# Five plain gate-and-up pairs instead of four ahead of the fast product, two of its four token sums on GpSimd, and another order on the queues

## The chip, the cores and the metric

One core of a Trainium2 chip. The metric is the device time of one launch in microseconds (us), as the median of several executions. TensorE multiplies; VectorE (DVE), ScalarE (ACT) and GpSimd (POOL) prepare its operands and take its results out of PSUM; SyncE (SP) issues the weight loads. Each engine works through its own queue in order, and waits on semaphores for the others.

## The reference

Two decoder layers on 512 tokens of width 1024, each layer wrapped by two half-step SwiGLU feed-forward networks (FFN 0 to 3), a convolution and sparse-attention mixer in the first, a gated DeltaNet mixer in the second. Only the FFNs are touched:

```python
def rmsnorm(x, gain):
    return x * lax.rsqrt(jnp.mean(x * x, axis=-1, keepdims=True) + NORM_EPS) * gain

def swiglu(h, w_gate, w_up, w_down):
    return (jax.nn.silu(h @ w_gate) * (h @ w_up)) @ w_down

x = x + 0.5 * swiglu(rmsnorm(x, norm_gain[layer, 0]), w_gate, w_up, w_down)   # D_FF = 2816
```

## The kernel before

Activations lie feature-major: 8 tiles of 128 features by 512 tokens. Each fp32 operand is split into a high part (a copy to fp32r, on ScalarE) and a low part (the difference, on VectorE, `split` and L1499), and each product is three matmuls, high by high, high by low and low by high. Weights come in units of 128 x 1024, four raw buffers deep: `load(n)` waits until the low part of unit n-3 is made.

An FFN has 22 pairs (gate and up, 128 columns of D_FF each), in two halves of 11, each half followed by 8 down units. A pair is computed in one of two ways:

- *plain*: two units (2p and 2p+1) of 8 x 3 matmuls of 512 tokens. The gain is folded into h, and rstd is applied after the product, so plain pairs can begin before rstd is known. `plain_gate` takes the gate product out of PSUM and scales it, `silu` on ScalarE, `plain_up` multiplies in two steps, `a_act` and `a_dve` split the result.
- *fast*: seven instead of eight block products (Strassen's scheme over two halves of features and two of tokens, with gate and up as the two column blocks), 7 parts of 4 x 3 matmuls of 256 tokens. It needs `hn`, the fully normed activations (`hn_dve`, 8 instructions), four sums of them, t_f[0] to t_f[3] (`t_sum`), their high parts t_hi (`t_act`) and low parts t_lo (`t_dve`), the high and low parts of hn itself, written over h_hi and h_lo (`b_act`, `b_dve`, three of each), and for each pair the sums of weights s_f (two on GpSimd, two on VectorE), with the high and low parts of ab, a22, s12 and s43.

`PLAIN` says how many pairs of each FFN are plain: 6, 4, 4, 4. They give VectorE and ScalarE time to make what the fast pairs need. That work is written by hand into the queues at fixed pairs: with `plain` pairs, hn behind the gate of pair plain-4, the t sums behind the gate of pair plain-3, t_lo around pair plain-2. On TensorE the sum of squares for the norm (`square_sum`, L609), which waits for GpSimd's adding up, stands ahead of unit 1 in FFNs 1 to 3 and ahead of unit 3 in FFN 0. ScalarE makes rstd from it (`norm`).

The first fast pair waits for the first part of h_lo (`b_ready`) before its first matmul, and for all four t_lo before its second part:

```python
pe.wait_ge(ab_ready, q + 1)
if new:
    pe.wait_ge(b_ready, 3 * f + 1)
part_product(own, ab_hi_w[ab], ab_lo_w[ab], 0, ...)
pe.wait_ge(s12_ready, q + 1)
if new:
    pe.wait_ge(t_ready, 4 * f + 4)
```

h_hi can be overwritten only when TensorE has read its first half in the last plain unit (`h_read`). t_lo[i] and t_f[i] are the same memory.

Of the kernel before, what the change touches and what calls it, by code (L numbers as in the profile page):

```python
# [10 lines left out]
ALU = mybir.AluOpType  # L11
# [59 lines left out]
PLAIN = (6, 4, 4, 4)  # L71
# [159 lines left out]
def program(nc, A, out):  # L231
    with ExitStack() as ctx:
# [187 lines left out]
        hn_made, tf_made, t_hi_made, t_ready = (sem(n) for n in ("hn_made", "tf_made", "t_hi_made", "t_ready"))  # L420
# [151 lines left out]
        def _(pe):  # L572
# [85 lines left out]
            def plain_pair(f, p):  # L658
# [3 lines left out]
                for u in range(2):  # L662
                    n = gate_unit(f, p) + u
                    bank = prod[:, 2 * (s % 2) + u, :]
                    if 2 * p + u == (1 if f else 3):
                        square_sum(norm_of(f))
# [376 lines left out]
        def _(act):  # L1043
# [92 lines left out]
            def t_act(f, i):  # L1136

                act.wait_ge(tf_made, 4 * f + (1, 2, 4, 3)[i])
                act.activation(t_hi[:, i], t_f[:, i], ACT.Copy, scale=-1.0 if i == 1 else 1.0).then_inc(t_hi_made, 1)
# [21 lines left out]
            def ffn_act(f):  # L1161
# [6 lines left out]
                for p in range(plain):  # L1168
# [3 lines left out]
                    if p == plain - 2:  # L1172
                        t_act(f, 2)
                    silu(f, p)
                    if p + 1 == plain:
                        break
                    if f or p:
                        split(n + 3)
# [3 lines left out]
                    a_act(f, p)  # L1182
                    if p == plain - 3:
                        t_act(f, 3)
                    if p == plain - 2:
                        ab_act(f, plain)
                        a22_act(f, plain)
                b_act(f, 0)
                s12_act(f, plain)
                for half in range(2):  # L1190
                    end = (half + 1) * HALF
                    for p in range((plain, HALF)[half], end):
                        s43_act(f, p)
                        if p == plain:
                            b_act(f, 1)
                        elif p != HALF:
                            a_act(f, p - 1)
                        snap_act(f, p, 0)
                        if p == plain:
                            b_act(f, 2)  # L1200
                            a_act(f, p - 1)
# [282 lines left out]
        def _(dve):  # L1484
# [103 lines left out]
            def t_sum(f, i):  # L1588


                if i == 0:
                    dve.wait_ge(hn_made, KT * (f + 1))
                    ins = dve.tensor_tensor(t_f[:, 0], hn[0][:, :, tokens(0)], hn[0][:, :, tokens(1)], ALU.subtract)
                elif i == 1:
                    dve.wait_ge(tf_made, 4 * f + 1)
                    ins = dve.tensor_tensor(t_f[:, 1], hn[1][:, :, tokens(1)], t_f[:, 0], ALU.add)
                elif i == 3:
                    ins = dve.tensor_tensor(t_f[:, 3], hn[1][:, :, tokens(1)], hn[0][:, :, tokens(1)], ALU.subtract)
                else:
                    dve.wait_ge(tf_made, 4 * f + 2)  # L1600
                    ins = dve.tensor_tensor(t_f[:, 2], t_f[:, 1], hn[1][:, :, tokens(0)], ALU.subtract)
                ins.then_inc(tf_made, 1)

            def t_dve(f, i):

                dve.wait_ge(t_hi_made, 4 * f + (1, 2, 4, 3)[i])
                dve.scalar_tensor_tensor(t_lo[:, i], t_f[:, i], -1.0 if i == 1 else 1.0, t_hi[:, i].bitcast(F32),
# [50 lines left out]
            def ffn_dve(f):  # L1658
                n0 = FFN_AT[f][0]
                plain = PLAIN[f]  # L1660
                for p in range(plain):
                    n = n0 + 2 * p
                    if p == plain - 2:
                        t_dve(f, 0)
# [9 lines left out]
                    elif p == plain - 3:  # L1674
                        t_sum(f, 0)
                        t_sum(f, 1)
                        t_sum(f, 3)
# [8 lines left out]
                    if p == plain - 4:  # L1686
                        hn_dve(f, range(KT // 2, KT // 2 + 1))
                    elif p == plain - 3:
                        t_sum(f, 2)
                    elif p == plain - 2:  # L1690
                        t_dve(f, 2)
                    a_dve(f, p)
                    if p == plain - 4:
                        hn_dve(f, range(KT // 2 + 1, KT))
                ab_dve(f, plain)
                sums_dve(f, plain)
                b_dve(f, 0)
                s12_dve(f, plain)
                a22_dve(f, plain)
# [594 lines left out]
```

## Time and profile before

| | |
|---|---|
| median of 3 runs | 2027.12 us (2026.6 to 2028.82) |
| the profiled execution | 2028.82 us |
| its span, first to last instruction | 2027.0 us |
| granted TensorE clock | 0.998 |
| TensorE (matmul) busy | 99% |
| VectorE busy | 69% |
| ScalarE busy | 49% |
| GpSimd busy | 26% |

Times in the rows below are us from the span's start, durations of one instruction in the groups are ns. Matmuls overlap in the records, so their pitch is read from start to start. An instruction of VectorE or ScalarE that is queued directly behind another begins some 0.1 us before that one's recorded end.

### The profile page before, as it was taken

The page shows a single profiled execution, that of the slowest core. Times are in us where ns is not written, and L with a number is a line of the kernel's source. Part 1 is how long each engine was busy: PE and PEld are TensorE (multiplying, and loading weights), DVE is VectorE, ACT ScalarE, POOL GpSimd, SP SyncE. Part 2 cuts the span into 40 slices and gives each one's busy share as a digit, 9 for nine tenths or more (in the row PEclk, how much of TensorE's full clock was granted, in tenths as well). Part 3 has the DMA queues.
Part 4 walks back from the last instruction along what each step waited for, and adds up shares of the span by engine and source line. Part 5 has one row for each costly group of instructions (what it writes and reads, how often), then busy time and mean ns, then how long its engine had stood idle before and what let it go on. Part 6 is the DMA issues. An engine that isn't in the chain of part 4 may idle for free.

```text
span 2027.0 us, 30533 instructions
## 1 busy us (share of the span) xinstructions
PE 1997.9 (99%) x12079; PEld 1777.4 (88%) x12079; DVE 1391.6 (69%) x1928; ACT 988.7 (49%) x1488; POOL 517.2 (26%) x530
## 2 busy tenths in 40 slices
PE   9999999999999999999999999999999999999998
PEld 7898998788888998998898999878888888989997
DVE  6955876588647955874894586376776548936863
ACT  5543653446745633553563364355565555624642
POOL 0201211454221301211130221156566011201211
PEclk9999999999999999999999999999999999999999
DMA  5232232444122232232232223122122122332231
GB/s 186 104 116 84 105 118 80 121 133 127 53 83 94 105 116 82 105 128 81 91 116 97 94 105 121 56 91 95 61 82 91 56 95 89 113 106 91 107 117 52
DMA packets 63167, 199.95 MB, mean 99 GB/s; under 512 B 12816, under 2 KB 14896, under 8 KB 63024
## 3 DMA queue, kind: packets, MB, share of 16 engines
q1 hardware_dynamic: 59616, 196.55, 28.0%
q8 instruction: 96, 1.57, 0.3%
q10 hardware_dynamic: 3408, 1.44, 0.3%
q14 instruction: 47, 0.39, 0.1%
HBM read 188.51 MB, written 2.38 MB: 94 GB/s over the span
## 4 chain that ended last, share of the span: by engine, by line
PE 87%; DVE 6%; ACT 3%; issue 2%; POOL 1%; DMA 1%; SPq 0%; ACTq 0%; DVEq 0%; POOLq 0%
PE prod L584 15%; PE prod L586 15%; PE prod L585 15%; PE misc L678 6%; PE misc L679 6%; PE misc L680 6%; PE prod L678 5%; PE prod L679 5%; PE prod L680 5%; PE misc L898 2%; PE misc L844 1%; DVE h_lo L1615 1%; ACT L1439 0%; ACT h_hi L1149 0%; PE misc L778 0%
## 5 line engine op out<-in xcount | busy, mean ns | idle before, releaser
L584 PE MATMUL prod<-a_hi,d_hi 128*128 128x512 f32 x693 | 269.7, 389 | 0.0
L585 PE MATMUL prod<-a_lo,d_hi 128*128 128x512 f32 x693 | 269.7, 389 | 0.0
L586 PE MATMUL prod<-a_hi,d_lo 128*128 128x512 f32 x693 | 269.6, 389 | 0.0
L2096 POOL TENSOR_TENSOR s_f<-raw 128x512 f32<-128x512 f32 x70 | 94.0, 1343 | 680.3 <-DVE s_lo L1574 361.2
L1499 DVE TENSOR_TENSOR d_lo<-raw,d_hi 128x1408 fp32r<-128x1408 f32 x64 | 104.0, 1626 | 238.2 <-ACT d_hi L1063 238.1
L1063 ACT ACTIVATE d_hi<-raw 128x1408 fp32r<-128x1408 f32 x64 | 88.3, 1379 | 220.0 <-PE prod L586 218.9
L2099 POOL TENSOR_TENSOR s_f<-raw 128x512 f32<-128x512 f32 x70 | 118.7, 1696 | 169.9 <-DVE s_lo L1579 169.9
L678 PE MATMUL prod<-t_hi,s_hi 128*128 128x256 f32 x560 | 158.9, 284 | 0.0
L680 PE MATMUL prod<-t_hi,s_lo 128*128 128x256 f32 x560 | 158.5, 283 | 0.0
L679 PE MATMUL prod<-t_lo,s_hi 128*128 128x256 f32 x560 | 158.5, 283 | 0.0
L586 PEld LDWEIGHTS prod<-a_hi,d_lo 128*128 128x128 f32 x693 | 130.1, 188 | 27.0
L584 PEld LDWEIGHTS prod<-a_hi,d_hi 128*128 128x128 f32 x693 | 130.1, 188 | 26.8
L585 PEld LDWEIGHTS prod<-a_lo,d_hi 128*128 128x128 f32 x693 | 130.1, 188 | 26.8
L584 PE MATMUL prod<-h_hi,ab_hi 128*128 128x512 f32 x368 | 151.7, 412 | 0.3 <-POOL ab_lo L2120 0.2
L584 PE MATMUL prod<-h_hi,s_hi 128*128 128x512 f32 x360 | 149.7, 416 | 2.0 <-DVE s_lo L1499 1.2
L586 PE MATMUL prod<-h_hi,ab_lo 128*128 128x512 f32 x368 | 144.0, 391 | 0.0
L585 PE MATMUL prod<-h_lo,ab_hi 128*128 128x512 f32 x368 | 143.5, 390 | 0.0
L1549 DVE TENSOR_TENSOR ab_lo<-raw,ab_hi 128x1024 fp32r<-128x1024 f32 x70 | 136.9, 1956 | 9.2 <-ACT ab_hi L1095 9.1
L1155 ACT ACTIVATE silu_g<-silu_g 128x512 f32<-128x512 f32 x88 | 55.6, 632 | 178.9 <-DVE silu_g L1639 156.8
L586 PE MATMUL prod<-h_hi,s_lo 128*128 128x512 f32 x360 | 141.0, 392 | 0.0
L585 PE MATMUL prod<-h_lo,s_hi 128*128 128x512 f32 x360 | 140.4, 390 | 0.0
L678 PEld LDWEIGHTS prod<-t_hi,s_hi 128*128 128x128 f32 x560 | 107.5, 192 | 0.3
(411 smaller groups left out, 5821.6 us busy)
## 6 DMA issues: line engine op xcount, KB each, us to landing
raw<-in_w SPq DMA_DIRECT2D x252, 512.0 KB, 3.3
raw<-in_wd SPq DMA_DIRECT2D x64, 704.0 KB, 4.1
blk<-blocks SPq DMA_DIRECT2D x16, 256.0 KB
x<-in_x SPq DMA_DIRECT2D x8, 256.0 KB, 5.9
k_dup<-k_dup SPq DMA_DIRECT2D x8, 256.0 KB, 3.5
silu_g<-g_rows SPq DMA_DIRECT2D x7, 256.0 KB, 4.8
out<-y_out SPq DMA_DIRECT2D x12, 128.0 KB, 2.0
raw<-in_w SPq DMA_DIRECT2D x4, 256.0 KB, 6.2
```

Of the source, the lines that this page charges most:

```text
L584: pe.matmul(bank, wh, hi, start=k == 0, stop=False)
L585: pe.matmul(bank, wh, lo, start=False, stop=False)
L586: ins = pe.matmul(bank, wl, hi, start=False, stop=k == tiles_n - 1)
L678: pe.matmul(bank, w_hi[:, at], hi[:, k, :], start=start and k == 0, stop=False, skip_group_check=not start)
L679: pe.matmul(bank, w_hi[:, at], lo[:, k, :], start=False, stop=False, skip_group_check=not start)
L680: ins = pe.matmul(bank, w_lo[:, at], hi[:, k, :], start=False, stop=k == KT // 2 - 1, skip_group_check=not start)
L1063: act.activation(weights(n)[0][:], raw[:, n % 4, 0:unit_width(n)], ACT.Copy).then_inc(hi_ready, 1)
L1155: act.activation(silu_g[:, s % 2, :], silu_g[:, s % 2, :], ACT.Silu).then_inc(silu_done, 1)
L1499: dve.tensor_tensor(w_lo[:], raw[:, n % 4, 0:unit_width(n)], w_hi[:].bitcast(F32), ALU.subtract)\
L1549: dve.tensor_tensor(ab_lo_w[ab][:], raw[:, n % 4, 0:2 * QUAD], ab_hi_w[ab][:].bitcast(F32), ALU.subtract)\
L2096: pool.tensor_tensor(s_f[:, 0, :], a21, a22, ALU.add).then_inc(s1_made, 1)
L2099: pool.tensor_tensor(s_f[:, 3, :], a11, a21, ALU.add).then_inc(s3_made, 1)
```

## The change

FFNs 1 to 3 get five plain pairs instead of four, with 17 fast ones. FFN 0 keeps six. In all four FFNs:

- t_f[3] and t_f[2] are made by GpSimd, ahead of its sums of weights, with a semaphore of their own. t_f[0] and t_f[1] stay on VectorE. t_lo[1] also waits for both of GpSimd's, since it overwrites t_f[1].
- hn: four behind the gate of pair plain-4, and four behind its a_lo.
- ScalarE, pair plain-3: t_hi[0] and t_hi[1] ahead of the split of the pair's second unit instead of behind it, t_hi[3] and t_hi[2] behind a_hi.
- VectorE: t_lo[0] behind a_lo of pair plain-3, t_lo[1] and t_lo[3] behind the gate of pair plain-2, then ab_lo of the first fast pair behind that pair's a_lo, t_lo[2] behind the first h_lo, ahead of the first fast pair.
- Around the first fast pair: a22 and s12 ahead of the first h_hi and h_lo on both engines, and s43 and the last plain pair's a ahead of the second and third.

In FFNs 1 to 3 the sum of squares stands on TensorE ahead of unit 2 instead of unit 1.

```diff
-PLAIN = (6, 4, 4, 4)
+PLAIN = (6, 5, 5, 5)
...
                 for u in range(2):
                     n = gate_unit(f, p) + u
-                    if 2 * p + u == (1 if f else 3):
+                    if 2 * p + u == (2 if f else 3):
                         square_sum(norm_of(f))
...
             def t_act(f, i):
-                act.wait_ge(tf_made, 4 * f + (1, 2, 4, 3)[i])
+                if i < 2:
+                    act.wait_ge(tf_made, 2 * f + i + 1)
+                else:
+                    act.wait_ge(tf_pool, 2 * f + (2, 1)[i - 2])
...
                     if p > (f == 0) and p + 1 < plain:
                         split(n + 2)
-                    if p == plain - 2:
-                        t_act(f, 2)
                     silu(f, p)
-                    if p + 1 == plain:
-                        break
-                    if f or p:
-                        split(n + 3)
                     if p == plain - 3:
                         t_act(f, 0)
                         t_act(f, 1)
-                    a_act(f, p)
+                    if p + 1 < plain:
+                        if f or p:
+                            split(n + 3)
+                        a_act(f, p)
                     if p == plain - 3:
                         t_act(f, 3)
+                        t_act(f, 2)
                     if p == plain - 2:
                         ab_act(f, plain)
-                        a22_act(f, plain)
+                a22_act(f, plain)
+                s12_act(f, plain)
                 b_act(f, 0)
-                s12_act(f, plain)
...
                         s43_act(f, p)
-                        if p == plain:
-                            b_act(f, 1)
-                        elif p != HALF:
+                        if p != HALF:
                             a_act(f, p - 1)
                         snap_act(f, p, 0)
                         if p == plain:
+                            b_act(f, 1)
                             b_act(f, 2)
-                            a_act(f, p - 1)
...
+            def t_sums(f):
+                dve.wait_ge(hn_made, KT * (f + 1))
+                dve.tensor_tensor(t_f[:, 0], hn[0][:, :, tokens(0)], hn[0][:, :, tokens(1)], ALU.subtract).then_inc(tf_made, 1)
+                dve.wait_ge(tf_made, 2 * f + 1)
+                dve.tensor_tensor(t_f[:, 1], hn[1][:, :, tokens(1)], t_f[:, 0], ALU.add).then_inc(tf_made, 1)
...
             def t_dve(f, i):
                 dve.wait_ge(t_hi_made, 4 * f + (1, 2, 4, 3)[i])
+                if i == 1:
+                    dve.wait_ge(tf_pool, 2 * f + 2)
...
                 for p in range(plain):
                     n = n0 + 2 * p
-                    if p == plain - 2:
-                        t_dve(f, 0)
...
                     elif p == plain - 3:
-                        t_sum(f, 0)
-                        t_sum(f, 1)
-                        t_sum(f, 3)
+                        t_sums(f)
...
                     plain_up(f, p)
-                    if p == plain - 4:
-                        hn_dve(f, range(KT // 2, KT // 2 + 1))
-                    elif p == plain - 3:
-                        t_sum(f, 2)
-                    elif p == plain - 2:
-                        t_dve(f, 2)
                     a_dve(f, p)
                     if p == plain - 4:
-                        hn_dve(f, range(KT // 2 + 1, KT))
-                ab_dve(f, plain)
+                        hn_dve(f, range(KT // 2, KT))
+                    elif p == plain - 3:
+                        t_dve(f, 0)
+                    elif p == plain - 2:
+                        ab_dve(f, plain)
                 sums_dve(f, plain)
+                a22_dve(f, plain)
+                s12_dve(f, plain)
                 b_dve(f, 0)
-                s12_dve(f, plain)
-                a22_dve(f, plain)
+                t_dve(f, 2)
...
+                        s43_dve(f, p)
+                        if p != HALF:
+                            a_dve(f, p - 1)
                         if p == plain:
                             b_dve(f, 1)
-                        s43_dve(f, p)
-                        if p == plain:
                             b_dve(f, 2)
-                        if p != HALF:
-                            a_dve(f, p - 1)
...
             def ffn_pool(f):
+                pool.wait_ge(hn_made, KT * (f + 1))
+                pool.tensor_tensor(t_f[:, 3], hn[1][:, :, tokens(1)], hn[0][:, :, tokens(1)], ALU.subtract).then_inc(tf_pool, 1)
+                pool.wait_ge(tf_made, 2 * f + 2)
+                pool.tensor_tensor(t_f[:, 2], t_f[:, 1], hn[1][:, :, tokens(0)], ALU.subtract).then_inc(tf_pool, 1)
```

## Rows read from the trace of the kernel before

**Rows 1.** The page: span, TensorE busy, granted clock, weight loads.

```profile
span 2027.0 us, 30533 instructions
...
PE 1997.9 (99%) x12079; PEld 1777.4 (88%) x12079; DVE 1391.6 (69%) x1928; ACT 988.7 (49%) x1488; POOL 517.2 (26%) x530
...
PEclk9999999999999999999999999999999999999999
...
raw<-in_w SPq DMA_DIRECT2D x252, 512.0 KB, 3.3
```

**Rows 2.** TensorE's waits: us in total, times, longest.

```profile
PE misc L678 <- DVE s_lo L1574: 5.0, 4, 1.3
```

**Rows 3.** Timeline of TensorE: plain pairs' first matmuls, FFNs 0 and 1.

```profile
32.37 0.39 PE L584 MATMUL prod<-h_hi,ab_hi 128*128 128x512 f32 x1
...
638.90 0.39 PE L584 MATMUL prod<-h_hi,s_hi 128*128 128x512 f32 x1
...
649.78 0.39 PE L584 MATMUL prod<-h_hi,s_hi 128*128 128x512 f32 x1
```

**Rows 4.** Timeline of TensorE: first matmuls of two adjacent fast pairs.

```profile
187.95 0.28 PE L678 MATMUL prod<-h_hi,ab_hi 128*128 128x256 f32 x1
...
198.03 0.28 PE L678 MATMUL prod<-h_hi,ab_hi 128*128 128x256 f32 x1
```

**Rows 5.** Timeline of TensorE, FFN 1: unit 0's last, sum, units 1 and 2.

```profile
620.88 0.39 PE L655 MATMUL prod<-h_lo,s_hi 128*128 128x512 f32 x1
621.60 1.12 PE L609 MATMUL misc<-sq_acc,consts 128*128 128x512 f32 x2 [0.34 <-POOL sq_acc L2083]
622.16 0.79 PE L584 MATMUL prod<-h_hi,ab_hi 128*128 128x512 f32 x1
...
628.02 0.39 PE L584 MATMUL prod<-h_hi,s_hi 128*128 128x512 f32 x1
```

**Rows 6.** Timeline of TensorE in FFN 1's second fast pair.

```profile
672.22 0.28 PE L680 MATMUL prod<-h_hi,ab_lo 128*128 128x256 f32 x1
673.77 0.39 PE L678 MATMUL misc<-t_hi,s_hi 128*128 128x256 f32 x1 [1.27 <-DVE s_lo L1574]
```

**Rows 7.** Timeline of ScalarE, FFN 1: Ln, Exp, table, silu, next split.

```profile
622.76 0.69 ACT L1086 ACTIVATE rstd<-misc,small 128x512 f32<-128x512 f32 x1 [0.34 <-PE misc L609]
623.48 0.63 ACT L1087 ACTIVATE rstd<-rstd 128x512 f32<-128x512 f32 x1
624.13 1.28 ACT L1167 ACT_TABLE_LOAD   x1
625.43 0.63 ACT L1155 ACTIVATE silu_g<-silu_g 128x512 f32<-128x512 f32 x1
628.28 1.06 ACT L1063 ACTIVATE ab_hi<-raw 128x1024 fp32r<-128x1024 f32 x1 [2.22 <-PE prod L586]
```

**Rows 8.** Timeline of VectorE, FFNs 0 and 1.

```profile
40.95 0.68 DVE L1623 TENSOR_TENSOR silu_g<-prod,rstd 128x512 f32<-128x512 f32 x1
...
624.83 2.73 DVE L1585 SCALAR_TENSOR_TENSOR hn<-x,small,rstd 128x512 f32<-128x512 f32 x4
...
655.63 0.68 DVE L1623 TENSOR_TENSOR silu_g<-prod,rstd 128x512 f32<-128x512 f32 x1
656.23 1.22 DVE L1549 TENSOR_TENSOR ab_lo<-raw,ab_hi 128x1024 fp32r<-128x1024 f32 x1
...
677.11 0.69 DVE L1655 TENSOR_TENSOR a_lo<-act_f,a_hi 128x512 fp32r<-128x512 f32 x1
677.71 2.32 DVE L1549 TENSOR_TENSOR ab_lo<-raw,ab_hi 128x1024 fp32r<-128x1024 f32 x1
```

**Rows 9.** Timeline of GpSimd in the same stretch, FFN 1.

```profile
677.27 1.68 POOL L2099 TENSOR_TENSOR s_f<-raw 128x512 f32<-128x512 f32 x1 [2.09 <-DVE s_lo L1579]
```

**Rows 10.** Groups by line and shape: busy us, mean ns of one.

```profile
L1095 ACT ACTIVATE ab_hi<-raw 128x1024 fp32r<-128x1024 f32 x70 | 73.5, 1051 | 0.0
...
L2120 POOL TENSOR_TENSOR s_lo<-raw,s_hi 128x1024 fp32r<-128x1024 f32 x13 | 31.1, 2389 | 30.7 <-ACT s_hi L1063 30.3
```

More of the change, by code:

```diff
@@ L418, in program @@
         act_seq, dve_seq = sem("act_seq"), sem("dve_seq")
-        hn_made, tf_made, t_hi_made, t_ready = (sem(n) for n in ("hn_made", "tf_made", "t_hi_made", "t_ready"))
+        hn_made, tf_made, tf_pool, t_hi_made, t_ready = (sem(n) for n in ("hn_made", "tf_made", "tf_pool", "t_hi_made", "t_ready"))
         h_read, b_hi_made, b_ready = sem("h_read"), sem("b_hi_made"), sem("b_ready")
@@ L1586, in hn_dve @@
                                              rstd[:], ALU.mult, ALU.mult).then_inc(hn_made, 1)
[L1588 to L1602, printed above, removed]
+            def t_sums(f):
[3 more added lines that the diff above has]
+                dve.tensor_tensor(t_f[:, 1], hn[1][:, :, tokens(1)], t_f[:, 0], ALU.add).then_inc(tf_made, 1)
             def t_dve(f, i):
                 dve.wait_ge(t_hi_made, 4 * f + (1, 2, 4, 3)[i])
+                if i == 1:
+                    dve.wait_ge(tf_pool, 2 * f + 2)
                 dve.scalar_tensor_tensor(t_lo[:, i], t_f[:, i], -1.0 if i == 1 else 1.0, t_hi[:, i].bitcast(F32),
```

## The prediction

> **What bounds the kernel now.** I read the page first: TensorE is busy for 1997.9 of 2027.0 us at the full granted clock [rows 1]. So only two things can move the time: the length of TensorE's own work, and stretches in which it waits. The list of TensorE's waits names the one wait that the changed code can touch four times: s_lo (L1574), 5.0 us in all [rows 2]. The timeline gives the pitches. A plain pair lasts 649.78 - 638.90 = 10.88 us [rows 3], so a unit of it 5.44; a fast pair lasts 198.03 - 187.95 = 10.08 us [rows 4]. At the norm, the sum matmul could have started at 620.88 + 0.23 = 621.11 and started at 621.60: 0.5 us of waiting for GpSimd's squares [rows 5]. In the second fast pair the next matmul came at 673.77 where 672.22 + 0.12 was due: 1.43 us [rows 6], once in each of the four FFNs, since rows 2 count four. Everything else at the change runs without a gap on TensorE, so the cover of each moved instruction has to be worked out from VectorE's, ScalarE's and GpSimd's queues.
>
> **Prices.** ScalarE: 1024 columns 1.05 us, 512 columns 0.63, table load 1.28 [rows 7, 10]. VectorE: 1024 columns 1.22, 512 columns 0.68; queued back to back it starts the next 0.08 earlier; four hn in 2.73 [rows 8]. GpSimd: 1024 columns with two inputs 2.39 [rows 10]. ScalarE starts a split 0.26 after the unit that frees its buffer (628.02 to 628.28) [rows 5, 7].
> The fourth price is a collision. s_lo's successor a_lo (L1655) runs on VectorE from 677.11 to 677.79; GpSimd's sum asks at 677.27 and ends at 678.95, 1.16 after that; VectorE's ab_lo asks at 677.71 and ends at 680.03, which is GpSimd's end plus 1.08 [rows 8, 9]. So two SBUF-reading instructions take turns, and the one that comes second waits for the whole of the first. I price each new collision so: the end of the other engine's instruction, plus 1.08 for VectorE, plus 2.25 for a GpSimd t sum.
> No row shows a collision with a GpSimd instruction of 1024 columns against these very tiles. The Trainium skill (SBUF — State Buffer, section "SBUF: two separate sides") says that GpSimd and a VectorE instruction with two SBUF inputs hold the shared port pair for a whole instruction; by it t_f[3] and t_f[2] on GpSimd block VectorE for up to 2.4 us each, which speaks against the change, and without it the change would come out near no difference. The trace agrees with it for the 512-column sums.
>
> **Part by part, FFNs 1 to 3.** Three fast pairs become plain: 3 x 0.80 = +2.4 us of pure TensorE work. The rest I follow in us from S, the start of the moved sum, which is now the end of unit 1.
> *Sum moved.* It no longer waits: -0.5. But rstd is now late: sum to Ln 1.16, to the end of Exp 2.51, table 3.81, silu of pair 0 4.46. Behind silu in ScalarE's queue stands the split of unit 3: 4.4 to 5.4; VectorE's low part 5.5 to 6.7. TensorE does unit 2 from 0.56 to 6.41 (5.86 after a sum [rows 5]) and starts unit 3 at 6.74: +0.33.
> *hn one pair later.* VectorE: up and a_lo of pair 0 to 9.4, low part of unit 4 9.7 to 10.9, gate 1 to 11.5, four hn to 14.15, unit 5 to 15.3, up 1 to 16.6, a_lo 17.3 to 18.0, four hn to 20.7, unit 6 to 21.8. Pair 2 starts at 12.18 and pair 3 is due at 23.06, so this is hidden, by 1.3 us.
> *t sums.* GpSimd's t_f[3] asks at 20.7, behind the low part of unit 6, and has the ports from 21.8 to 24.05. VectorE does gate 2 (its product is in PSUM) to 22.4 and then t_f[0] waits: 25.1 instead of 23.5. t_f[1] to 26.4. On ScalarE t_hi[0] and t_hi[1] now stand ahead of the split of unit 7: t_hi[1] 26.4 to 27.45, split to 28.4. Meanwhile GpSimd's t_f[2] has the ports from 26.4 to 28.8, so the low part of unit 7 ends at 29.9. It is due at 23.06 + 5.44 = 28.50 and TensorE starts it at 29.95: +1.45.
> *Its echo.* up 2 to 31.2, then ScalarE in order: a_hi, t_hi[3], t_hi[2], split of unit 8 to 34.8; VectorE waits for GpSimd's first s_f sum (its weights land 3.3 us [rows 1] after unit 7's low part) and ends at 36.0. Unit 8 was due at 35.4: +0.65.
> *Last plain pair.* It starts at 36.03, call it X. VectorE: gate 3 (0.6 us), t_lo[1] behind a GpSimd sum (to X+2.2), t_lo[3] 3.3, unit 9 4.5, up 3 5.8, a_lo, then ab_lo, which now stands here and waits for ab_hi until 7.4: to 8.7; gate 4 to 9.3, where its product was there from X+5.7 (before, the last gate started at 655.63 [rows 8], 5.85 after its pair's start). Then s_f[1] to 9.9, and on ScalarE silu, a22_hi, s12_hi to 11.5 and only then h_hi to 12.45; on VectorE h_lo to 13.9. The first fast pair needs h_lo and was due at X+10.9: +3.0. Before, h_hi stood ahead of s12_hi and this was hidden.
> *First fast pair.* t_lo[2] now stands behind h_lo, and GpSimd's next s_f sum gets the ports first: it ends 2.2 after h_lo, 0.8 later than part 2 of the pair can use it: +0.8. Then up 4, s43_lo, a_lo and again a GpSimd sum before the second h_lo: part 5 waits 1.0. The second fast pair's s12_lo is then ready 0.4 us before its use, so the old 1.43 goes.
> Sum for one FFN: +0.80 + 0.33 + 1.45 + 0.65 + 3.0 + 0.8 + 1.0 - 0.5 - 1.43 = +6.1; three: 18.3.
>
> **FFN 0** keeps its six plain pairs and its sum. It has the same order of t sums. Its gate before hn comes 40.95 - 32.37 = 8.6 us after its pair's start [rows 3, 8], 10.25 in the others, so VectorE is further ahead and unit 9 waits 0.9 instead of 1.45: 0.9 + 0.65 + 3.0 + 0.8 + 1.0 - 1.43 = +4.9.
> Total +23.2 us. The profiled execution took 2028.82 (span 2027.0 and 1.8 around it), 0.08% above the median 2027.12; on the median's footing 2050.3.
>
> **Bounds of what is not seen.** If no collision costs anything, t_f[0] ends at 23.5 and unit 7 is in time; the last pair is then late only by its own chain. Without the echo, VectorE's last gate still starts 6.7 after its pair (a_hi, ab_hi and ab_lo come before it) and h_lo ends at 11.9: +1.07. One FFN: 0.80 + 0.33 + 1.07 - 0.5 - 1.43 = +0.3, FFN 0 -0.4: total +0.5. If collisions cost but the early lateness doesn't appear, the 0.8 and 1.0 come on top: 4 x 1.8 more, +7.7. Upwards, if GpSimd's 2.39 us falls once more on a chain that is already late, each FFN loses up to another 1.5 to 2: +6 to 8.
>
> **Rivals.**
> 1. *Slack wins (faster).* The extra plain pair gives VectorE 10.9 us for 4.8 us of added work (two low parts, a gate, an up in two steps, an a_lo) and takes two sums of 1.22 off it. If every stall went, what is left is +2.4 - 3 x 0.5 - 4 x 1.43 = -4.8: 2022.3. For it: VectorE has no idle gap of note in the 10 us before the stall now. It decides where h_lo ends under 10.9 after the last plain pair's start; worked in order, the best that I find is 11.9, so 0.12.
> 2. *No collisions (no difference).* +0.5: 2027.6. Against it are rows 8 and 9. 0.12.
> 3. *The echo is absent.* GpSimd's t_f[3] falls into a gap of VectorE: +7.7, 2034.8. For it: one instruction's order decides. 0.14.
> The forecast, late queues in front of both the split of unit 7 and the first fast pair: 0.62.
> The clock is not a rival: it is granted in full in all 40 slices, through the stalls of now [rows 1].
>
> **Numbers.** This kernel's measurement tells about 0.2% (4 us) from nothing. Faster 0.12, from rival 1; within 0.2% 0.10, most of rival 2; slower 0.78. The forecast's own range is 2040 to 2057 (a third of the stalls fewer; another 2 us in each FFN). The range reaches down to rival 3 and a little under, 2030 to 2057, and leaves out rivals 1 and 2.
>
> **What would show it.** TensorE waiting for a low part L1499 once or twice ahead of each first fast pair, each wait 0.5 to 1.5 us; a wait of about 3 us of the first fast pair's first matmul for h_lo; waits of part 2 for t_lo and of part 5 for h_lo; no wait for s_lo L1574 in the second fast pair; the sum matmul without a wait; t_f[0] on VectorE lengthened to 2.5 to 3 us. I am wrong if t_f[0] keeps 1.22 us beside GpSimd's t_f[3], or if the first fast pair starts 10.9 us after the last plain pair in all four FFNs: then the extra pair's slack has paid.

## The result, and the profile after

| | median us | runs, range | profiled span |
|---|---|---|---|
| before | 2027.19 | 4, 2026.6 to 2028.82 | 2027.0 |
| after | 2049.31 | 4, 2048.34 to 2050.57 | 2049.0 |

The ratio is 1.0110, with a 95% interval from 1.0098 to 1.0122: slower, by 22 us. The profiled execution of the changed kernel took 2050.8 us.

The page of the changed kernel, the lines that answer to [rows 1]:

```profile
span 2049.0 us, 30259 instructions
...
PE 2008.3 (98%) x11971; PEld 1780.7 (87%) x11971; DVE 1377.8 (67%) x1908; ACT 980.4 (48%) x1473; POOL 529.8 (26%) x532
...
PEclk9999999999999999999999999999999999999999
```

TensorE is busy for 10.4 us more, in 108 matmuls less, and the span is 22.0 us longer: part of the loss is waiting, and part of it is matmuls that took longer. The clock row still shows nines only, since a slice is 51 us long.

TensorE's largest waits (us in total, times, longest) in the changed kernel. The wait for s_lo L1574 of [rows 2] is not among them any more:

```profile
PE prod L678 <- DVE h_lo L1607: 10.7, 4, 2.7
PE prod L584 <- DVE s_lo L1498: 4.1, 6, 1.2
PE prod L584 <- DVE ab_lo L1498: 4.1, 4, 1.3
```

The timeline of TensorE in FFN 1 (start, duration, instruction, and in brackets the idle time and what ended it), from the end of unit 1 to the first fast pair:

```profile
630.26 0.39 PE L586 MATMUL prod<-h_hi,ab_lo 128*128 128x512 f32 x1
630.49 1.02 PE L609 MATMUL misc<-sq_acc,consts 128*128 128x512 f32 x2
...
636.61 0.39 PE L586 MATMUL prod<-h_hi,s_lo 128*128 128x512 f32 x1
637.11 0.50 PE L584 MATMUL prod<-h_hi,ab_hi 128*128 128x512 f32 x1
...
658.78 0.39 PE L586 MATMUL prod<-h_hi,s_lo 128*128 128x512 f32 x1
660.36 0.50 PE L584 MATMUL prod<-h_hi,ab_hi 128*128 128x512 f32 x1 [1.20 <-DVE ab_lo L1498]
...
666.54 0.47 PE L584 MATMUL prod<-h_hi,s_hi 128*128 128x512 f32 x1 [0.43 <-DVE s_lo L1498]
...
677.28 0.39 PE L586 MATMUL prod<-h_hi,ab_lo 128*128 128x512 f32 x1
680.37 0.36 PE L678 MATMUL prod<-h_hi,ab_hi 128*128 128x256 f32 x1 [2.70 <-DVE h_lo L1607]
680.81 0.42 PE L678 MATMUL prod<-h_hi,ab_hi 128*128 128x256 f32 x1
```

Matmuls of a plain unit start 0.23 us apart. So the moved sum starts on time, unit 3 is 637.11 - 636.61 - 0.23 = 0.27 us late, unit 7 660.36 - 658.78 - 0.23 = 1.35, unit 8 (666.54) 0.59, and the first fast pair 680.37 - 677.28 - 0.23 = 2.86. Here and below a wait is counted so, from start to start; the figure in brackets is somewhat smaller. The last line begins what was not expected: matmuls of a fast pair start 0.12 us apart [rows 6], and from here on they start about 0.21 apart.

Windows of FFN 1 in the changed kernel: length, busy time of PE, PEld, DVE, ACT and POOL with counts, then the granted clock, the DMA share and GB/s. The first is the wait, the second begins 0.4 us after its end, and the third is the stretch after that:

```profile
677.50:680.30 2.80, 0.16 (x1) 0.00 (x0) 2.60 (x4) 2.22 (x3) 1.04 (x1) 1.00 0.56 173
680.76:684.16 3.40, 3.40 (x18) 3.40 (x17) 3.37 (x4) 0.37 (x1) 0.59 (x1) 0.50 0.27 108
684.20:690.00 5.80, 5.80 (x49) 5.65 (x48) 5.62 (x6) 4.61 (x8) 1.68 (x1) 1.00 0.00 0
```

TensorE was idle for 2.7 us, and 0.4 us after it had begun again its granted clock was 0.50, the 1.2 GHz level, for 3.4 us. At 0.12 us apart it would have started 28 matmuls in that time. It started 16 (the row counts two more that were under way), so 12 fewer, or some 1.5 us of matmuls. This happened in all four FFNs of this execution. With three plain pairs more (2.4) it accounts for 8.4 of the 10.4 us by which TensorE is busier; the rest was not taken apart. A fifth such stretch lies outside the FFNs: in the DeltaNet mixer TensorE waited 3.03 us for t_inv at 1377.98 us (2.39 before), and around the end of that wait the granted clock was 0.50 for 6.8 us, where it stayed at 1.00 before.

Why unit 7 and the first fast pair were late is in the other queues. VectorE, FFN 1:

```profile
652.65 2.82 DVE L1590 TENSOR_TENSOR t_f<-hn 128x1024 f32<-128x1024 f32 x1
...
658.81 1.50 DVE L1498 TENSOR_TENSOR ab_lo<-raw,ab_hi 128x1024 fp32r<-128x1024 f32 x1 [2.08 <-ACT ab_hi L1063]
...
677.86 1.23 DVE L1573 TENSOR_TENSOR s_lo<-s_f,s_hi 128x1024 fp32r<-128x1024 f32 x1 [0.20 <-ACT s_hi L1113]
679.00 1.22 DVE L1607 TENSOR_TENSOR h_lo<-hn,h_hi 128x1024 fp32r<-128x1024 f32 x1
680.14 2.30 DVE L1599 SCALAR_TENSOR_TENSOR t_lo<-t_f,t_hi 128x1024 fp32r<-128x1024 f32 x1
```

ScalarE:

```profile
655.51 1.06 ACT L1142 ACTIVATE t_hi<-t_f 128x1024 fp32r<-128x1024 f32 x1 [2.10 <-DVE t_f L1590]
656.77 1.06 ACT L1142 ACTIVATE t_hi<-t_f 128x1024 fp32r<-128x1024 f32 x1 [0.20 <-DVE t_f L1592]
657.73 1.04 ACT L1063 ACTIVATE ab_hi<-raw 128x1024 fp32r<-128x1024 f32 x1
...
676.78 1.04 ACT L1113 ACTIVATE s_hi<-s_f 128x1024 fp32r<-128x1024 f32 x1
677.73 1.04 ACT L1152 ACTIVATE h_hi<-hn 128x1024 fp32r<-128x1024 f32 x1
```

GpSimd:

```profile
651.14 3.25 POOL L2074 TENSOR_TENSOR t_f<-hn,hn 128x1024 f32<-128x1024 f32 x1 [25.64 <-DVE hn L1584]
656.81 2.41 POOL L2076 TENSOR_TENSOR t_f<-t_f,hn 128x1024 f32<-128x1024 f32 x1 [2.42 <-DVE t_f L1592]
```

GpSimd's t_f[3] ends at 654.39, and VectorE's t_f[0] ends 1.08 later, at 655.47, as [rows 8, 9] show it for a pair of 512 and 1024 columns. With it t_hi[0], t_hi[1], the split behind them (657.73) and the low part at 658.81 are late. The low part takes 1.50 instead of 1.22, because t_f[2] ends at 659.22, again 1.09 before it. In front of the first fast pair s12_hi (676.78) stands ahead of h_hi (677.73), and h_lo ends at 680.22; the pair starts at 680.37.

By the Trainium skill (SBUF — State Buffer, section "SBUF: two separate sides") GpSimd and a VectorE instruction with two SBUF inputs share one port pair, and whichever starts first holds it for its whole instruction, if GpSimd's reads SBUF. The 2.82 us of t_f[0] agree with that.

### The profile page after: what moved, and what is told of

Same layout as the page of the kernel before. It is cut to its first block, busy times and chain, and to the rows that moved or that the text cites. A ratio compares the mean times of both kernels' runs of the same rounds, so it can differ in the third digit from the quotient of the medians.

```text
span 2049.0 us, 30259 instructions
## 1 busy us (share of the span) xinstructions
PE 2008.3 (98%) x11971; PEld 1780.7 (87%) x11971; DVE 1377.8 (67%) x1908; ACT 980.4 (48%) x1473; POOL 529.8 (26%) x532
## 4 chain that ended last, share of the span: by engine, by line
PE 83%; DVE 8%; ACT 4%; issue 3%; POOL 1%; DMA 1%; SPq 0%; ACTq 0%; DVEq 0%; POOLq 0%
PE prod L584 13%; PE prod L586 13%; PE prod L585 13%; PE misc L678 6%; PE misc L679 6%; PE misc L680 6%; PE prod L678 5%; PE prod L680 5%; PE prod L679 5%; PE misc L898 2%; DVE hn L1584 1%; PE misc L844 1%; DVE t_f L1590 1%; DVE act_f L1624 1%; DVE act_f L1621 0%
## 5 line engine op out<-in xcount | busy, mean ns | idle before, releaser
L2085 POOL TENSOR_TENSOR s_f<-raw 128x512 f32<-128x512 f32 x67 | 91.2, 1361 | 579.6 <-DVE s_lo L1573 351.7
L584 PE MATMUL prod<-h_hi,ab_hi 128*128 128x512 f32 x392 | 161.4, 412 | 4.7 <-DVE ab_lo L1498 4.1
L584 PE MATMUL prod<-h_hi,s_hi 128*128 128x512 f32 x384 | 161.0, 419 | 5.0 <-DVE s_lo L1498 4.1
L2088 POOL TENSOR_TENSOR s_f<-raw 128x512 f32<-128x512 f32 x67 | 111.6, 1666 | 162.9 <-DVE s_lo L1578 162.9
L586 PE MATMUL prod<-h_hi,ab_lo 128*128 128x512 f32 x392 | 153.5, 392 | 0.0
L585 PE MATMUL prod<-h_lo,ab_hi 128*128 128x512 f32 x392 | 153.1, 390 | 0.0
L678 PE MATMUL prod<-t_hi,s_hi 128*128 128x256 f32 x536 | 152.0, 284 | 0.0
L680 PE MATMUL prod<-t_hi,s_lo 128*128 128x256 f32 x536 | 151.9, 283 | 0.0
L586 PE MATMUL prod<-h_hi,s_lo 128*128 128x512 f32 x384 | 151.0, 393 | 0.0
L585 PE MATMUL prod<-h_lo,s_hi 128*128 128x512 f32 x384 | 150.6, 392 | 0.0
L680 PEld LDWEIGHTS prod<-t_hi,s_lo 128*128 128x128 f32 x536 | 103.1, 192 | 0.0
```

What stands on the lines that cost most here:

```text
L584: pe.matmul(bank, wh, hi, start=k == 0, stop=False)
L585: pe.matmul(bank, wh, lo, start=False, stop=False)
L586: ins = pe.matmul(bank, wl, hi, start=False, stop=k == tiles_n - 1)
L678: pe.matmul(bank, w_hi[:, at], hi[:, k, :], start=start and k == 0, stop=False, skip_group_check=not start)
L680: ins = pe.matmul(bank, w_lo[:, at], hi[:, k, :], start=False, stop=k == KT // 2 - 1, skip_group_check=not start)
L2085: pool.tensor_tensor(s_f[:, 0, :], a21, a22, ALU.add).then_inc(s1_made, 1)
```

## The experiments

Each kernel is compared with the kernel before, measured beside it: 2027.42 us (7 runs) beside e1 to e4, 2028.28 (15) beside e5 to e8, 2028.23 (18) beside e9 to e12. The runs stand here by what they ask, not in the order of their numbers. Three possible causes of the waits were set against each other: the order around the first fast pair, the order of the splits, and GpSimd's hold on VectorE. Where a waits list is shown, its totals are of the idle time as the profile gives it, over the whole kernel.

**e1. Order around the first fast pair.** The changed kernel with ScalarE and VectorE in the old order there. ScalarE goes in the same way, but its a22_hi stays behind the last silu; the second and third h_hi and h_lo go back too:

```diff
+                    if p == plain - 2:
+                        t_dve(f, 2)
                     a_dve(f, p)
...
-                    elif p == plain - 2:
-                        ab_dve(f, plain)
+                ab_dve(f, plain)
                 sums_dve(f, plain)
-                a22_dve(f, plain)
-                s12_dve(f, plain)
                 b_dve(f, 0)
-                t_dve(f, 2)
+                s12_dve(f, plain)
+                a22_dve(f, plain)
...
```

> The changed kernel, with the order of before around the first fast pair on both queues (first h_hi ahead of s12_hi, ab_lo and first h_lo behind the last gate, t_lo[2] back in pair plain-2, the later h_lo interleaved as before). Theory (late queues in front of the first fast pair): its wait falls from 2.9 to about 0.9 us, the stretch at the lower granted clock behind it vanishes (1.8 us), the wait for s12_lo in the second fast pair comes back with about 1 us: 4 x -2.8, so 2038. Rival (the extra pairs and GpSimd's sums are the cost, not the order): within 2 us of 2049.

Measured: 2041.76 us, ratio 1.0070 (1.0053 to 1.0087), span 2039.5. TensorE's waits:

```profile
PE misc L678 <- DVE s_lo L1575: 5.0, 4, 1.3
...
PE prod L678 <- DVE h_lo L1609: 2.5, 4, 0.6
```

The wait ahead of the first fast pair falls from 2.86 to between 0.76 and 0.79, no slow stretch follows, and units 3, 7 and 8 wait as they did (0.27, 1.33, 0.59). The old wait of [rows 2] comes back whole, at 1.42 and not at the 1.0 expected, which accounts for 1.7 of the 3.8 us of the miss. That the slow stretch was priced at 1.8 and not at 1.5 accounts for 1.2 more. The new order costs 7.6 us by the medians (9.5 by the spans of two single executions), net of that wait.

**e2. Only the first h_hi and h_lo and ab_lo moved back.** As the run above, without the move of t_lo[2] and without that of the second and third h_lo:

```diff
-                s12_act(f, plain)
                 b_act(f, 0)
+                s12_act(f, plain)
...
-                a22_dve(f, plain)
-                s12_dve(f, plain)
                 b_dve(f, 0)
+                s12_dve(f, plain)
+                a22_dve(f, plain)
                 t_dve(f, 2)
```

> The changed kernel, with only the first h_hi and h_lo moved ahead of s12 and a22 and ab_lo behind the last gate, t_lo[2] left ahead of the fast pairs. Theory (what counts is VectorE's whole queue up to s12_lo of the second fast pair, not one instruction's place): the first wait falls from 2.9 to 0.4 us, but part 2 then waits some 2.6 us for t_lo[2] and later parts 0.5 to 1, in sum 3.8 against 4.7 us, so 2046, or 2049 if the wait for t_lo[2] also brings the lower clock. Rival (h_lo's place alone was the cost): 4 x -4.3, so 2032.

Measured: 2047.86 us, ratio 1.0100 (1.0085 to 1.0115), span 2047.3. TensorE's largest wait:

```profile
PE misc L678 <- DVE t_lo L1599: 9.2, 4, 2.3
```

The first matmul waits 0.44 only, and part 2, which needs t_lo[2], waits 2.45. The clock fell behind that wait in two of the four FFNs, and the time lies between the two that were expected. h_lo's place is not the cause by itself: with t_lo[2] left in the queue in front of the pair, that queue is too long, and the last of it is waited for.

**e3. The split ahead of t_hi.** The changed kernel with

```diff
                     silu(f, p)
+                    if p + 1 < plain:
+                        if f or p:
+                            split(n + 3)
                     if p == plain - 3:
                         t_act(f, 0)
                         t_act(f, 1)
                     if p + 1 < plain:
-                        if f or p:
-                            split(n + 3)
                         a_act(f, p)
```

> The changed kernel, with ScalarE's split of the second unit ahead of t_hi[0] and t_hi[1] again in pair plain-3. Theory (the order of ScalarE's queue makes the wait for the unit in pair plain-2): both waits of TensorE for L1498 there go, 1.36 and 0.59 us in FFNs 1 and 3, a little more in FFN 2, 1.6 in FFN 0, in sum 7.5 to 8.5: 2041.5. Rival (GpSimd's hold of the ports makes it, whatever ScalarE's order): at least 2046.

Measured: 2046.94 us, ratio 1.0093 (1.0078 to 1.0109), span 2044.9. Unit 7's wait is gone, and unit 8, which was 0.59 late, is now 2.09 late. GpSimd and VectorE of this kernel:

```profile
656.25 3.31 POOL L2077 TENSOR_TENSOR t_f<-t_f,hn 128x1024 f32<-128x1024 f32 x1 [2.42 <-DVE t_f L1593]
```

```profile
657.93 2.17 DVE L1625 TENSOR_TENSOR act_f<-act_f,rstd 128x512 f32<-128x512 f32 x1
```

t_f[2] ends at 659.56. Where it held the low part of unit 7 in the changed kernel, it now holds the second step of up (2.17 us), and behind that come a_hi, t_hi and the split of unit 8. The expectation of 2041.5 missed this, and its rival, at least 2046, was right: the order of the split chooses who pays for the collision, and does not remove it.

**e4. The t sums on VectorE.** The changed kernel with t_f[3] and t_f[2] behind t_f[1] on VectorE and none on GpSimd:

```diff
                 dve.tensor_tensor(t_f[:, 1], hn[1][:, :, tokens(1)], t_f[:, 0], ALU.add).then_inc(tf_made, 1)
+                dve.tensor_tensor(t_f[:, 3], hn[1][:, :, tokens(1)], hn[0][:, :, tokens(1)], ALU.subtract).then_inc(tf_pool, 1)
+                dve.wait_ge(tf_made, 2 * f + 2)
+                dve.tensor_tensor(t_f[:, 2], t_f[:, 1], hn[1][:, :, tokens(0)], ALU.subtract).then_inc(tf_pool, 1)
```

> The changed kernel, with t_f[3] and t_f[2] made by VectorE behind t_f[1]. Theory (the two instructions of 2.4 us on GpSimd hold VectorE up by more than the 2.3 us that they take off it): t_f[0] back to 1.2 us, the first wait (1.36) gone, the second 0.35: about 6 us less, 2043.5. Rival (they relieve VectorE): slower than 2049, by up to 2 us in each FFN.

Measured: 2043.25 us, ratio 1.0077 (1.0062 to 1.0092), span 2040.0.

```profile
PE prod L678 <- DVE h_lo L1610: 10.7, 4, 2.7
```

Unit 7's wait is gone with the t_hi still ahead of the split, unit 8's falls to 0.29, and the 2.85 in front of the first fast pair stays. So the waits of the splits come from GpSimd's two sums, and the wait for h_lo doesn't. The clock fell behind that wait in FFNs 0 and 1 only.

**e10. The sums alone, in the kernel before.** t_f[3] and t_f[2] on GpSimd, all else as before:

```diff
-                elif i == 3:
-                    ins = dve.tensor_tensor(t_f[:, 3], hn[1][:, :, tokens(1)], hn[0][:, :, tokens(1)], ALU.subtract)
-                else:
-                    dve.wait_ge(tf_made, 4 * f + 2)
-                    ins = dve.tensor_tensor(t_f[:, 2], t_f[:, 1], hn[1][:, :, tokens(0)], ALU.subtract)
...
             def ffn_pool(f):
+                pool.wait_ge(hn_made, KT * (f + 1))
+                pool.tensor_tensor(t_f[:, 3], hn[1][:, :, tokens(1)], hn[0][:, :, tokens(1)], ALU.subtract).then_inc(tf_pool, 1)
+                pool.wait_ge(tf_made, 2 * f + 2)
+                pool.tensor_tensor(t_f[:, 2], t_f[:, 1], hn[1][:, :, tokens(0)], ALU.subtract).then_inc(tf_pool, 1)
```

> The kernel before, with t_f[3] and t_f[2] made by GpSimd and nothing else. Theory (each holds VectorE's next instruction with two SBUF inputs for up to 2.4 us): t_f[0] takes 2.8 us, the second step of up about 2.2, the last gate starts some 0.9 us later, and the first fast pair waits up to 1 us: +1 to +5, so 2030.5. Rival (2.3 us less on VectorE shorten its queue): the wait of 1.43 in the second fast pair shrinks, 2024 or less.

Measured: 2035.32 us, ratio 1.0032 (1.0020 to 1.0044), span 2031.3. VectorE and TensorE in FFN 1:

```profile
637.81 2.82 DVE L1596 TENSOR_TENSOR t_f<-hn 128x1024 f32<-128x1024 f32 x1
...
643.66 2.17 DVE L1632 TENSOR_TENSOR act_f<-act_f,rstd 128x512 f32<-128x512 f32 x1
```

```profile
651.80 0.47 PE L584 MATMUL prod<-h_hi,s_hi 128*128 128x512 f32 x1 [1.00 <-DVE s_lo L1502]
```

The same 2.82 and 2.17 us, and one plain unit in each FFN is some 1.1 us late. Theory and sign are right, and the size is missed: 7.1 us above before, where +1 to +5 was expected. Taking two sums of 1.2 us off VectorE lengthened t_f[0] by 1.6 and up by 1.5: GpSimd gave back more than it took. The profiled execution was the shortest of six, 4.3 us above before by its span; the late units account for that much, and the rest of the 7.1 is open.

**e5, e11. The sum of squares.** The changed kernel with the sum back at unit 1 (e5, below), and the kernel before with the sum at unit 2 (e11, the reverse):

```diff
-                    if 2 * p + u == (2 if f else 3):
+                    if 2 * p + u == (1 if f else 3):
```

> The changed kernel, with the sum of squares ahead of unit 1 again in FFNs 1 to 3. Theory (the moved sum gains its wait of 0.5 us, and loses it again through the late split of unit 3 and later hn): the sum waits 0.5 us again, the wait of 0.27 for unit 3 goes, the wait for unit 7 falls from 1.36 to about 0.9: 3 x -0.2, so 2048.5, no difference that tells. Rival (the late rstd is the root of all the later waits): unit 7, unit 8 and the first fast pair in time, 2035 or less.

Measured: 2049.57 us, ratio 1.0106 (1.0093 to 1.0120), span 2047.1; the sum waits 0.50 again, unit 7 0.99 instead of 1.35, the first fast pair 2.83. No difference, as expected.

> The kernel before, with the sum of squares ahead of unit 2 in FFNs 1 to 3 and nothing else. Theory (four pairs have no room for an rstd 5.9 us later; the fifth pair is what pays for the move): waits of 0.3 to 0.9 us for two or three low parts in each of FFNs 1 to 3 and a later first fast pair, against 0.5 gained: +4 to +9, about 2033. Rival (the moved sum is free, as in the changed kernel): 2025.8.

Measured: 2035.6 us, ratio 1.0036 (1.0022 to 1.0049), span 2033.8.

In FFN 1 the units behind the sum wait 0.70, 0.35 and 0.72 and the first fast pair 0.77, and the old 1.42 stays. With four plain pairs a norm that comes 5.4 us later reaches as far as the first fast pair; in the changed kernel the fifth pair and the waits that were there anyhow take this in. The same edit costs 7.4 us in one kernel and nothing that tells in the other.

**e6, e7. The number of plain pairs.** The kernel before with five (e6, below), and the changed kernel with four (e7, the reverse):

```diff
-PLAIN = (6, 4, 4, 4)
+PLAIN = (6, 5, 5, 5)
```

> The kernel before, with PLAIN = (6, 5, 5, 5) and nothing else. Theory (a plain pair costs 0.80 us more than a fast one, and the wait in the second fast pair stays, since it comes from work behind the last gate): +2.4, so 2029.6. Rival (the extra pair's time absorbs the waits of 1.43 us): 2025.3.

Measured: 2030.16 us, ratio 1.0009 (1.0000 to 1.0018), span 2028.8. The second fast pair waits for s_lo L1574 four times, 5.0 us in all, as in [rows 2].

> The changed kernel, with PLAIN = (6, 4, 4, 4). Theory (the later rstd leaves too little room, so this order of the queues needs the fifth plain pair): -2.4 for the pairs, but more waits for low parts, hn now directly behind the late rstd, 2049 to 2056. Rival (the extra plain pairs are a plain cost): 2046.9.

Measured: 2055.18 us, ratio 1.0131 (1.0116 to 1.0147), span 2054.8; FFN 1 waits 0.70, 0.98, 2.50, 1.93, 0.72 and 0.81. Where nothing needs them, the three pairs cost 1.9 us by the medians, with an interval from 0 to 3.7. The traces are sharper: from the first fast pair of FFN 0's second half to that of FFN 1's it is 604.95 us before and 605.74 in e6, and from there to that of FFN 2's 347.96 and 348.76, so 0.80 us for each pair, as was worked out. They leave the wait of [rows 2] as it was. Within the rest of the change they are worth 5.9 us, or 4.8 if each kernel is taken against the kernel before beside it.

**e9. Three parts undone.** The changed kernel with the edits of e1, e3 and e4 together. Of the change there stay the five plain pairs, the moved sum, hn in two fours one pair later, t_f[2], t_hi[2] and t_lo[0] ahead of their old places, and a22_hi behind its own.

> The changed kernel, with the order around the first fast pair as before, ScalarE's split ahead of t_hi[0] and t_hi[1], and all four t sums on VectorE: what stays of the change is the fifth plain pair, the moved sum and hn in two fours. Theory (the loss lies in those three, and what stays costs the pairs' 2.4 us and next to nothing more): 1.5 to 3.5 us above before, about 2030. Rival (something of the loss hangs on the moved sum or hn's place): more than 5 us above before.

Measured: 2034.85 us, ratio 1.0033 (1.0020 to 1.0049), span 2033.0.

```profile
649.04 1.21 DVE L1593 TENSOR_TENSOR t_f<-hn 128x1024 f32<-128x1024 f32 x1
...
659.79 1.22 DVE L1501 TENSOR_TENSOR s_lo<-raw,s_hi 128x1024 fp32r<-128x1024 f32 x1 [1.02 <-ACT s_hi L1063]
```

t_f[0] takes 1.21 us without a GpSimd sum beside it. FFN 1 still waits 0.27, 0.31, 0.76 and 1.42, so FFNs 1 to 3 lose 0.80 + 0.27 + 0.31 + 0.76 - 0.5 = 1.64 each and FFN 0 its 0.76: 5.7 us, where 6.0 is measured between the spans. The rival of this expectation was right. The three edits account for 14.5 of the 22.1 us by the medians (16.0 of 22.0 by the spans). What stays is slower than before too. FFN 0 has the 0.76 us as well, with its six pairs and its sum where it was, so neither the fifth pair nor the moved sum makes it. The trace points at t_hi[2]: together with t_hi[3] it now stands ahead of the split of unit 8 on ScalarE, and VectorE idles for 1.02 us ahead of that low part (the last line), 1.01 in FFN 0, where before it did not idle there. No run put t_hi[2] back, so this is not shown.

**e8, e12. Against the old wait of the second fast pair.** Two tries in the kernel before. In e8, s12_lo goes ahead of a22_lo and of the late a_lo, in the fast pair plain:

```diff
                             sums_dve(f, p + 1)
-                            a22_dve(f, p + 1)
-                            s12_dve(f, p + 1)
+                            if p == plain:
+                                s12_dve(f, p + 1)
+                                a22_dve(f, p + 1)
+                                a_dve(f, p - 1)
+                            else:
+                                a22_dve(f, p + 1)
+                                s12_dve(f, p + 1)
```

> The kernel before, with s12_lo of the second fast pair ahead of its a22_lo, and a_lo of the last plain pair behind both. Theory (the wait of 1.43 us is VectorE's queue from the first fast pair's start to that s12_lo): s12_lo ends 1.2 us earlier (0.6 each for a22_lo and a_lo; GpSimd's sum now holds up ab_lo instead), 4 x -1.2, so 2022.4. Rival (another instruction comes last, or a_lo is missed elsewhere): 2027 or more.

Measured: 2039.79 us, ratio 1.0053 (1.0041 to 1.0066), span 2038.4. TensorE's largest wait, two instructions of ScalarE, and the windows behind the wait in FFN 1:

```profile
PE prod L678 <- ACT snap_a L1129: 8.7, 4, 2.2
```

```profile
679.47 0.61 ACT L1159 ACTIVATE a_hi<-act_f 128x512 fp32r<-128x512 f32 x1
679.99 0.36 ACT L1129 ACTIVATE snap_a<-prod 128x256 f32<-128x256 f32 x1
```

```profile
680.30:684.00 3.70, 3.60 (x18) 3.60 (x19) 3.70 (x4) 2.39 (x5) 1.67 (x1) 0.55 0.00 0
```

The wait falls from 1.43 to 0.71 as meant, and a larger one, 2.32 us, comes 5.3 us after it. The late a_lo delays VectorE's next gate and up; with them a_hi is late on ScalarE; and behind a_hi stands the snapshot of a PSUM bank that TensorE needs. That is 2.3 us in each FFN, with the clock at its lower level behind it (0.55 is the mean of a window somewhat longer than the slow stretch).

In e12, s12_lo stays where it was, a_lo goes a whole fast pair later, and the snapshot ahead of a_hi:

```diff
-                        elif p != HALF:
-                            a_act(f, p - 1)
                         snap_act(f, p, 0)
+                        if p != plain and p != HALF:
+                            a_act(f, p - 1)
...
-                        if p != HALF:
+                        if p == plain + 1:
+                            a_dve(f, plain - 1)
+                        if p != HALF and p != plain:
                             a_dve(f, p - 1)
```

> The kernel before, with a_lo of the last plain pair one fast pair later on VectorE, and ScalarE's first snapshot of a fast pair ahead of the a_hi of the pair before. Theory (the 1.43 us are VectorE's queue up to s12_lo of the second fast pair, and the wait for the snapshot that the late a_lo brought was a_hi's place in ScalarE's queue): the wait in the second fast pair falls to 0.8, no wait for the snapshot: 4 x -0.6, so 2.5 us below before. Rival (the wait reappears one pair later): no difference.

Measured: 2025.78 us, ratio 0.9988 (0.9979 to 0.9997), span 2022.8.

```profile
PE misc L678 <- DVE s_lo L1574: 2.6, 4, 0.7
```

The wait is 0.82 in all four FFNs instead of 1.43, and none takes its place. This is the fastest kernel of the study, 2.45 us under the kernel before, as expected. It is a small gain, with an interval that ends just below 1, and under the 0.2% that the prediction set as its bound.

## Why the prediction was right, and where it was wrong

The forecast was 2050.3 us, with a range from 2030 to 2057, and 2049.31 was measured. Its terms, in us:

| term | predicted | measured | shown by |
|---|---|---|---|
| three plain pairs | +2.4 | +2.4 by the traces | e6 |
| sum's own wait | -0.5 | -0.5 | trace after; e5 |
| unit 3 | 0.33 | 0.27 | trace after |
| unit 7 | 1.45 | 1.35 | e3, e4 |
| unit 8 | 0.65 | 0.59; in FFN 2 1.49 | e3, e4 |
| first fast pair, h_lo | 3.0 | 2.86 | e1, e2 |
| part 2 for t_lo, part 5 for h_lo | 0.8 + 1.0 | slow matmuls, 1.5; at the full clock 0.72 + 0.82 | e3, e4 |
| old wait gone | -1.43 | -1.43 | e1 |
| FFN 0, unit 9 | 0.9 | 0.99 | trace after |

Over the FFNs 0 to 3 the measured terms come to 4.5, 5.4, 6.3 and 5.4, together 21.6; the spans differ by 22.0, and 23.2 was predicted. The queues ran as the prediction had worked them out: from S (630.49), t_f[0] ends at 24.98 (25.1 predicted) and the low part of unit 7 at 29.82 (29.9).

- **Hidden moves.** hn one pair later was costed at nothing, and FFN 1 has no wait between unit 3 and unit 7: right in the changed kernel. With three parts undone (e9), 0.31 us ahead of a plain unit and 0.76 ahead of the first fast pair remain. What makes the 0.76 is open (see e9), and this step didn't foresee it.
- **Collision.** GpSimd's t_f[3] lengthens t_f[0] to 2.82 us (2.5 to 3 predicted), and t_f[2] the low part of unit 7. The runs with the sums on VectorE, and with the sums alone on GpSimd, show cause and size from both sides.
- **The echo in FFN 2.** There unit 8 is 1.49 late and not 0.65. GpSimd's first sum of weights came just ahead of the low part, as VectorE and GpSimd show:

```profile
1018.78 2.10 DVE L1498 TENSOR_TENSOR ab_lo<-raw,ab_hi 128x1024 fp32r<-128x1024 f32 x1 [1.02 <-ACT ab_hi L1063]
```

```profile
1018.51 1.29 POOL L2085 TENSOR_TENSOR s_f<-raw 128x512 f32<-128x512 f32 x1 [5.68 <-issue]
```

- **Last plain pair.** h_lo as the last of a queue that is too long: right, with 2.86 for 3.0. e2 shows that moving h_lo alone only makes t_lo[2] the one that is waited for. e1 shows that the wait shortens, by 2.1 us, when t_lo[2] too goes back to where the queue has room for it, a pair earlier.
- **The step that failed: "The clock is not a rival".** It rested on the 40 slices of [rows 1], and a slice, 51 us long, doesn't show a slow stretch of 3.4 us. The kernel before has one too, at its very start, around the end of a wait of 1.76 us:

```profile
8.80:12.20 3.40, 3.21 (x8) 2.54 (x9) 3.40 (x6) 3.29 (x6) 0.00 (x0) 0.50 1.02 360
```

The change brings waits of 2.83 to 2.86 us in the FFNs, and behind them the clock fell. The 0.8 and 1.0 us that were to be waited for in parts 2 and 5 did not appear as such: with matmuls at half speed, t_lo and h_lo were in time. Instead of 1.8 us of waiting there were some 1.5 us of slow matmuls, so the sum came out right by a partly wrong way. The run with the sums on VectorE shows that one takes the place of the other. The clock fell behind the first fast pair's wait in its FFN 1 and not in its FFN 2, and from that pair's start to the first fast pair of the second half it is 798.98 - 676.88 = 122.10 us in the one and 1150.82 - 1028.71 = 122.11 in the other:

```profile
676.88 0.55 PE L678 MATMUL prod<-h_hi,ab_hi 128*128 128x256 f32 x1 [2.69 <-DVE h_lo L1610]
...
798.98 0.28 PE L678 MATMUL prod<-h_hi,ab_hi 128*128 128x256 f32 x1
...
1028.71 0.35 PE L678 MATMUL prod<-h_hi,ab_hi 128*128 128x256 f32 x1 [2.68 <-DVE h_lo L1610]
...
1150.82 0.28 PE L678 MATMUL prod<-h_hi,ab_hi 128*128 128x256 f32 x1
```

The changed kernel takes 122.11 there, and e6, with the old wait of 1.43 and no slow stretch, 122.15. So the slow matmuls added nothing to the waits that they displaced, and either costs here what the old wait had cost. The run with the split ahead of t_hi shows why. Its FFN 0 waited 2.37 and kept the full clock, and there the two waits stand, 0.72 for t_lo and 0.81 for h_lo, where 0.8 and 1.0 were predicted. Its part 5 starts 86.69 - 79.26 = 7.43 us after the pair, and in the changed kernel, with slow matmuls and no such waits, 687.79 - 680.37 = 7.42. So VectorE's second h_lo sets that start either way, and the matmuls at the lower clock use up the room in front of it. That it uses no more is luck: in FFN 2 of e5, where the clock fell only 1.5 us after the pair had started and part 2 had already waited 0.71, the same stretch lasts 122.38. The start of part 5 in the changed kernel, then TensorE in FFN 0 of e3, and the windows of e3 in FFN 0 and in FFN 1, where the clock fell:

```profile
687.79 0.39 PE L678 MATMUL misc<-h_hi,ab_hi 128*128 128x256 f32 x1
```

```profile
79.26 0.36 PE L678 MATMUL prod<-h_hi,ab_hi 128*128 128x256 f32 x1 [2.20 <-DVE h_lo L1608]
...
81.48 0.36 PE L678 MATMUL misc<-t_hi,s_hi 128*128 128x256 f32 x1 [0.56 <-DVE t_lo L1600]
...
86.69 0.39 PE L678 MATMUL misc<-h_hi,ab_hi 128*128 128x256 f32 x1 [0.66 <-DVE h_lo L1608]
```

```profile
79.30:83.00 3.70, 3.14 (x25) 2.96 (x26) 3.67 (x4) 0.31 (x1) 0.96 (x1) 1.00 0.35 144
...
679.40:683.00 3.60, 3.60 (x18) 3.60 (x19) 3.56 (x4) 0.26 (x1) 0.90 (x1) 0.53 0.32 131
```

- **Rivals.** "Slack wins" and "no collisions" are out by the collisions and by h_lo at 2.86. Rival 3, without the echo, is out by units 7 and 8; the run with the sums on VectorE is the one nearest to it, at 2043.25 and not 2034.8, since the 2.85 stays there. The fifth pair does give slack, 4.8 to 5.9 us worth, but only within this order.

## What to carry to other kernels

An engine off the critical path that takes an SBUF sum from a busier one must be priced by what it holds up as well as by what it takes: here, with nothing else changed (e10), 2.4 us taken off VectorE for each FFN came back as 3.1 on two of its other instructions. When a queue ahead of a deadline is too long, swapping two items in it only changes which operand is waited for (e2). Look for the item that can go a whole stage earlier or later, where the queue has room (e1, e12), and check what stands behind it in every in-order queue (e8). A wait of 2 us and more on TensorE may be followed by slow matmuls, which a page with 40 slices doesn't show. What they cost depends on what TensorE would have waited for behind them: nothing more in the changed kernel, and some 1.5 us for each FFN in e8, where it would have waited for nothing.

## What the hardware did that was not expected

Behind a wait of 2.0 to 2.9 us in an FFN TensorE's granted clock was in many cases 0.50, the 1.2 GHz level, for 3.4 us, and 1.00 after that; matmuls of a fast pair then started 0.21 us apart instead of 0.12. (Windows that are a little longer than the slow stretch give 0.53 to 0.55.) The stretch began between 0.5 us before the wait's end and 1.5 us after it. It never followed the waits of 1.41 to 1.43 us in the second fast pair. At the start of the kernel it came with waits of 1.5 to 1.9 us in some runs, the kernel before among them, and not in others.

The length of the wait alone doesn't decide it. Behind 2.83 to 2.86 us the clock fell in all four FFNs of the changed kernel, in three of four with the sum of squares early (e5) and in two of four with the sums on VectorE (e4); behind 2.45 in two of four (e2); behind 2.33 in all four (e8). In e3 it fell behind 2.33 and not behind 2.37 and 2.82, and behind a late plain unit at 2.01 and not at 2.09. What else decides it is open.
